# Packing gate columns and rank columns of an input projection into one weight tile

## The reference, cut to what matters

```
p_ctx = h_ctx @ w_in          # 256 x 1024 by 1024 x 3936
p_lat = h_lat @ w_in          # the same for the 256 tokens
u = concatenate([p_ctx, p_lat])
mq, mk, rr, rk, rv, mv, mo, gates, lw_f, lw_b, la, lg = split(u)
# widths: 7 x 512, gates 32, lw_f 64, lw_b 64, la 64, lg 128
li_f = gates[0] + b_i[0];   lf_f = log_sigmoid(gates[1] + b_f[0])   # 8 heads each
li_b = gates[2] + b_i[1];   lf_b = log_sigmoid(gates[3] + b_f[1])
a = sigmoid(a0 + la @ a_b_mat)       # la is the rank-64 input of this product
g = sigmoid(lg) @ g_b_mat            # lg is used for the 256 tokens alone
```

## Time and profile before

| | us |
|---|---|
| median of three runs | 2305.46 |
| lowest and highest run | 2303.93, 2309.15 |
| span of the profiled execution, first to last instruction | 2302.1 |
| TensorE busy in it | 2104.5 (91%) |
| VectorE, ScalarE, GpSimd busy | 793.3, 427.9, 38.1 |
| mean granted TensorE clock | 0.942 |

### The profile page before, as it was taken

The page is one execution under the profiler, slowest core; times in us unless marked ns, Lnnn a source line. Parts: engine busy times, 40 slices in busy tenths (PEclk is TensorE's granted clock), DMA queues, the critical chain, the costliest instruction groups (busy, mean ns, idle before and its releaser), DMA issues.

```text
span 2302.1 us, 31821 instructions
## 1 busy us (share of the span) xinstructions
PE 2104.5 (91%) x13702; PEld 1457.2 (63%) x13702; DVE 793.3 (34%) x1639; ACT 427.9 (19%) x892; POOL 38.1 (2%) x34
## 2 busy tenths in 40 slices
PE   6999886887899999999899899999898889999998
PEld 4554664677744444444575678887777778648844
DVE  3494488555411111111234345424674320001001
ACT  2200243221311111111233310003322110000001
POOL 1000200000000000000000000000000000000000
PEclk9999896688999999999998999999998889999999
DMA  9610004204579999999744278753300077899696
GB/s 311 244 37 1 1 1 148 74 2 161 198 323 426 427 422 428 427 428 425 271 153 175 73 274 324 275 214 110 111 1 2 1 276 273 312 394 345 247 345 239
DMA packets 161862, 511.95 MB, mean 222 GB/s; under 512 B 9022, under 2 KB 32269, under 8 KB 149069
## 3 DMA queue, kind: packets, MB, share of 16 engines
q1 hardware_dynamic: 146352, 480.51, 54.2%
q10 hardware_dynamic: 15389, 29.67, 3.5%
HBM read 509.11 MB, written 1.05 MB: 222 GB/s over the span
## 4 chain that ended last, share of the span: by engine, by line
PE 83%; DVE 7%; ACT 4%; DMA 3%; issue 2%; SPq 0%; POOL 0%; ACTq 0%; DVEq 0%; POOLq 0%
PE PS L388 35%; PE PS L2406 10%; PE PS L2427 5%; PE PS L2560 4%; PE PS L2321 4%; PE PS L2332 4%; PE PS L2245 3%; DMA work<-in_moe_w_gate_up_dram 2%; PE PS L2511 2%; PE PS L857 1%; PE PS L629 1%; PE PS L849 1%; PE PS L637 1%; PE PS L1668 1%; DMA work<-in_w_ada_dram 1%
## 5 line engine op out<-in xcount | busy, mean ns | idle before, releaser
L388 PE MATMUL PS<-hT,work 128*128 128x256 f32 x1456 | 329.0, 386 | 4.5 <-ACT hT L919 4.0
L388 PEld LDWEIGHTS PS<-hT,work 128*128 128x128 f32 x1456 | 278.4, 193 | 50.7 <-issue 10.1
L388 PE MATMUL PS<-work 128*128 128x256 f32 (+4 forms) x960 | 284.0, 457 | 2.4 <-DVE work L1976 1.5
L388 PEld LDWEIGHTS PS<-work 128*128 128x128 f32 (+2 forms) x960 | 178.6, 187 | 105.8 <-issue 78.3
L2406 PE MATMUL PS<-work,sq 128*64 128x512 f32 x1024 | 222.6, 592 | 1.3 <-ACT sq L2350 1.3
L388 PE MATMUL PS<-sq,work 128*128 128x128 f32 x1408 | 162.9, 280 | 11.7 <-DMA work<-in_moe_w_gate_up_dram 11.7
L388 PEld LDWEIGHTS PS<-sq,work 128*128 128x128 f32 x1408 | 162.5, 197 | 13.7 <-DMA work<-in_moe_w_gate_up_dram 12.7
L2406 PEld LDWEIGHTS PS<-work,sq 128*64 128x64 f32 x1024 | 76.0, 137 | 144.5 <-issue 144.5
L2427 PE MATMUL PS<-work 128*64 128x512 f32 x512 | 113.4, 595 | 12.0 <-ACT work L2444 12.0
L2560 PE MATMUL PS<-work 128*64 128x512 f32 (+1 forms) x352 | 114.4, 593 | 2.0 <-ACT work L2590 2.0
L2388 DVE COPY work<-PS 128x1024 f32<-128x1024 f32 x22 | 26.9, 1225 | 232.4 <-PE PS L2427 119.1
(11 more groups left out here) (584 smaller groups left out, 2304.9 us busy)
## 6 DMA issues: line engine op xcount, KB each, us to landing
work<-in_ex_gate_dram SPq DMA_DIRECT2D x32, 2048.0 KB, 12.3
work<-in_ex_up_dram SPq DMA_DIRECT2D x32, 2048.0 KB, 15.4
work<-in_ex_down_dram SPq DMA_DIRECT2D x32, 2048.0 KB, 11.0
work<-in_moe_w_gate_up_dram SPq DMA_DIRECT2D x32, 2048.0 KB, 10.6
work<-in_moe_w_down_dram SPq DMA_DIRECT2D x16, 2048.0 KB, 14.5
work<-in_ada_w_dram ACTq DMA_DIRECT2D x14, 2048.0 KB, 11.4
work<-in_moe_w_gate_up_dram SPq DMA_DIRECT2D x16, 1536.0 KB, 13.4
work<-in_ada_w_dram SPq DMA_DIRECT2D x10, 2048.0 KB, 11.6
```

The source lines that it names most:

```text
L388: ins = pe.matmul(outp, lhs, rhs, start=n == 0, stop=n == len(pairs) - 1, **kw)
```

## The change

The two gate copies and la's 64 weight columns are laid into one weight tile of 128 columns. It has four groups of 32 columns: input gates forward, input gates backward, forget gates forward, forget gates backward. The first 8 columns of a group are gate heads, the next 16 are a quarter of la's columns, the last 8 zeros. One product makes one output tile of 128 rows, and ScalarE reads it three times: rows 0 to 39 to li, rows 64 to 103 to lf, all 128 rows to la. A scale per row (1 on gate rows, 0 elsewhere) keeps the rank rows out of li and lf. `w_a` gets 128 rows, laid out like the tile with zeros on the gate rows and the padding, so that `la` in the new layout multiplies it directly; it is loaded by four DMAs of 16 rows, after a fill with zeros. The other two tiles stay as they are; `N_GATE` becomes 3, and counts that depend on it are renumbered.

```diff
-    w_a = sb("w_a", [C, H * C])
+    w_a = sb("w_a", [P, H * C])
-    w_gate = sb("w_gate", [P, KT, 2, 40])
+    w_gate = sb("w_gate", [P, KT, P])
-    gate_bias = sb("gate_bias", [40, 2])
+    gate_bias = sb("gate_bias", [P, 2])
-    for name, spec in (("w_in", ["act"] * 5 + ["dve"] * 20 + ["act"] * 8), ...
+    for name, spec in (("w_in", ["act"] * 3 + ["dve"] * 20 + ["act"] * 8), ...
-    N_GATE = 5
+    N_GATE = 3
-                act.dma_start(gate_bias[32 * d:32 * d + 8, j:j + 1], A[name]...)
+                act.dma_start(gate_bias[64 * j + 32 * d:64 * j + 32 * d + 8, 0:1], A[name]...)
-        ld(w_a[:, :], A["r_aB"][0])
+        sp.wait_ge(S["zeroed"], 4)
+        for g in range(4):
+            ld(w_a[32 * g + 8:32 * g + 24, :], A["r_aB"][0][16 * g:16 * g + 16, :])
-        eng.wait_ge(S["later"], 16 * 11)
+        eng.wait_ge(S["later"], 16 * 14)
     def stage0_pool():
-        pool.memset(w_gate[:, :, :, :], 0.0).then_inc(S["zeroed"], 1)
-        pool.memset(gate_bias[:, :], 0.0).then_inc(S["zeroed"], 1)
+        pool.memset(w_gate[:, :, :], 0.0).then_inc(S["zeroed"], 1)
+        po.link(pool.memset(gate_bias[:, :], 0.0))
+        for g in range(4):
+            po.link(pool.memset(gate_bias[32 * g:32 * g + 8, 1:2], 1.0))
+        pool.memset(w_a[:, :], 0.0).then_inc(S["zeroed"], 1)
     def gate_weights_pool():
-                ins = pool.tensor_copy(w_gate[:, :, j, 32 * d:32 * d + 8], w[:, :, 16 * d + 8 * j:16 * d + 8 * j + 8])
+                g = 2 * j + d
+                pool.tensor_copy(w_gate[:, :, 32 * g:32 * g + 8], w[:, :, 16 * d + 8 * j:16 * d + 8 * j + 8])
+                ins = pool.tensor_copy(w_gate[:, :, 32 * g + 8:32 * g + 24], w[:, :, 160 + 16 * g:160 + 16 * g + 16])
     def w_in_pe():
-        for j in range(2):
-            o = tile_begin("w_in", j)
-            product(o[0:40, :], [(w_gate[:, k, j, :], hall[:, k, :]) for k in range(KT)]).then_inc(S["tile_full"], 1)
+        product(tile_begin("w_in", 0), [(w_gate[:, k, :], hall[:, k, :]) for k in range(KT)]).then_inc(S["tile_full"], 1)
-        for j, (c0, m, t0, n) in enumerate(((32, P, 0, 2 * N), (160, C, 0, 2 * N), (224, P, N, N))):
+        for j, (c0, t0, n) in enumerate(((32, 0, 2 * N), (224, N, N))):
     def w_in_act():
-            evac(j, dst[0:40, :], tile_full(act, "w_in", j)[0:40, :], ACT.Identity, bias=gate_bias[:, j:j + 1])
-        evac(2, lw, tile_full(act, "w_in", 2), ACT.Tanh)
-        evac(3, la[0:C, :], tile_full(act, "w_in", 3)[0:C, :], ACT.Copy)
-        evac(4, lg, tile_full(act, "w_in", 4)[:, 0:N], ACT.Sigmoid)
+            rows_ = slice(C * j, C * j + R40)
+            act.activation(dst[0:R40, :], o[rows_, :], ACT.Identity, bias=gate_bias[rows_, 0:1], scale=gate_bias[rows_, 1:2])
+        evac(0, la, o, ACT.Copy)
+        evac(1, lw, tile_full(act, "w_in", 1), ACT.Tanh)
+        evac(2, lg, tile_full(act, "w_in", 2)[:, 0:N], ACT.Sigmoid)
     # two waits for tile 33 dropped beside a wait for the same count; emptied counts 2 -> 1, 13 -> by the list
-                product(o, [(w_a[:, p * P:(p + 1) * P], la[0:C, :])]).then_inc(S["tile_full"], 1)
+                product(o, [(w_a[:, p * P:(p + 1) * P], la)]).then_inc(S["tile_full"], 1)
```

More of the change, by code:

```diff
@@ L337, in build @@
     first_tile = {}
-    for name, spec in (("w_in", ["act"] * 5 + ["dve"] * 20 + ["act"] * 8), ("kap", ["act"] * 4), ("lora", ["act"] * 16),
+    for name, spec in (("w_in", ["act"] * 3 + ["dve"] * 20 + ["act"] * 8), ("kap", ["act"] * 4), ("lora", ["act"] * 16),
                        ("bonus", ["dve"] * 4), ("w_out", ["dve"] * 8), ("mla", ["act"] * 7 + ["dve"]),
@@ L420, in param_rows_act @@
                 row_loads[0] += 1
-                act.dma_start(gate_bias[32 * d:32 * d + 8, j:j + 1], A[name][0, d:d + 1, :].rearrange("a h -> h a"))\
+                act.dma_start(gate_bias[64 * j + 32 * d:64 * j + 32 * d + 8, 0:1], A[name][0, d:d + 1, :].rearrange("a h -> h a"))\
                    .then_inc(S["rows"], 16)
@@ L964, in w_in_pe @@
         pe.wait_ge(S["zeroed"], 5)
-        for j in range(2):
-            o = tile_begin("w_in", j)
-            product(o[0:40, :], [(w_gate[:, k, j, :], hall[:, k, :]) for k in range(KT)]).then_inc(S["tile_full"], 1)
+        product(tile_begin("w_in", 0), [(w_gate[:, k, :], hall[:, k, :]) for k in range(KT)]).then_inc(S["tile_full"], 1)
         w = unit(place["w_in", 7], KT, 352)
-        for j, (c0, m, t0, n) in enumerate(((32, P, 0, 2 * N), (160, C, 0, 2 * N), (224, P, N, N))):
-            o = tile_begin("w_in", 2 + j)
-            product(o[0:m, 0:n], [(w[:, k, c0:c0 + m], hall[:, k, t0:t0 + n]) for k in range(KT)])\
+        for j, (c0, t0, n) in enumerate(((32, 0, 2 * N), (224, N, N))):
+            o = tile_begin("w_in", 1 + j)
+            product(o[:, 0:n], [(w[:, k, c0:c0 + P], hall[:, k, t0:t0 + n]) for k in range(KT)])\
                 .then_inc(S["tile_full"], 1)
@@ L1032, in w_in_act @@
         act.wait_ge(S["rows"], 16 * row_loads[0])
+        o = tile_full(act, "w_in", 0)
         for j, dst in enumerate((li, lf)):
-            evac(j, dst[0:40, :], tile_full(act, "w_in", j)[0:40, :], ACT.Identity, bias=gate_bias[:, j:j + 1])
-        evac(2, lw, tile_full(act, "w_in", 2), ACT.Tanh)
-        evac(3, la[0:C, :], tile_full(act, "w_in", 3)[0:C, :], ACT.Copy)
-        evac(4, lg, tile_full(act, "w_in", 4)[:, 0:N], ACT.Sigmoid)
+            rows_ = slice(C * j, C * j + R40)
[3 more added lines that the diff above has]
+        evac(2, lg, tile_full(act, "w_in", 2)[:, 0:N], ACT.Sigmoid)
         ada_act(N_FIRST)
@@ L1088, in ml_pool @@
     def ml_pool():
-        pool.wait_ge(S["tile_full"], first_tile["w_in"] + 33)
         pool.wait_ge(S["tile_full"], first_tile["w_in"] + N_GATE + 28)
@@ L1095, in ml_gate_log_dve @@
     def ml_gate_log_dve():
-        dve.wait_ge(S["emptied_act"], 2)
+        dve.wait_ge(S["emptied_act"], 1)
         dve.scalar_tensor_tensor(out=g40(z_), in0=g40(lf), scalar=-1.0, in1=g40(lf), op0=ALU.mult, op1=ALU.max).then_inc(S["ml_args"], 1)
@@ L1188, in ml_tokens_dve @@
         dve.wait_ge(S["tile_full"], first_tile["w_in"] + N_GATE + 28)
-        dve.wait_ge(S["tile_full"], first_tile["w_in"] + 33)
         dve.tensor_tensor(diag[0:R40], over(ident[0:R40, 0:R40], 4), along(g40(decay), R40), ALU.mult)\
@@ L1469, in ml_out_dve @@
         dve.wait_ge(S["hn_std"], 3)
-        dve.wait_ge(S["emptied_act"], 13)
+        dve.wait_ge(S["emptied_act"], tile_owner[first_tile["w_in"] + N_GATE + 27][1])
         dv.link(dve.tensor_tensor(hm, hm, hv, ALU.mult))
```

## The result

| | before | changed |
|---|---|---|
| median of 20 executions each | 2308.21 us | 2300.73 us |
| lowest and highest | 2303.34, 2319.19 | 2292.46, 2308.84 |
| ratio of the changed to before | | 0.9959, 95% interval 0.9948 to 0.9970 |
| span of the profiled execution | 2302.1 us | 2299.1 us |
| mean granted clock in it | 0.942 | 0.938 |

The change makes the kernel 0.41% faster, 9.5 us by the ratio; 13.7 was forecast. The median of 2300.73 lies above the range of 2287.0 to 2297.0. With all executions of the study taken together (39 of the changed kernel, 117 of before) the means are 2299.8 and 2309.5 us, a difference of 9.7 with a standard error of 0.9.

A forecast was written before the change was run, and what follows sets the result against it. TensorE was taken to bound the input projection without a break. Span 2302.1 less 13.7 us of removed passes gives 2288.4; with 3.4 carried over to the median, 2291.7 us, range 2287.0 to 2297.0.

The forecast's parts named there:

- The work removed: Input projection on TensorE: two of four full-width passes, 32 load/matmul pairs, go; 13.7 us saved, bounds 13.5 and 13.8.
- What hides the added steps: Before and around the projection: added DMAs, fills, copies and readings stay under slack, 7.3 us for mq weights; nothing lost.
- the sign that copies or fills were not covered: TensorE's first projection matmul later than 49.6 us would mean the added GpSimd copies or fills delayed it.
- The scaled reading: ScalarE's li and lf readings with a per-row scale: between 0.68 us and twice that each, no change to the total.
- D: VectorE's convolution does not start earlier and holds TensorE; only the 2.2 us of slack is kept: 2303.3 us, chance 0.05.
- E: Four short w_a DMAs stall SP's queue, so mq weights come late and TensorE waits 19.9 us: 2311.6 us, chance 0.04.
- C: Wider weight loads are exposed in tile 0, costing 1.1 us, or 1.5 at low clock: 2293.2 us, chance 0.04.
- Later: After the projection: wider w_a products cost nothing, and events of the chain release the rest, so the gain stays whole.
- Rival B: Downstream of the projection, low-clock stretches fall differently, one costing 3.1 us: 2294.8 or 2288.6 us, chance 0.15.
- B's own sign: A gain of 13.7 us at 226 us that has become another number by 560 us.
- The sum's base: Whole kernel: the span of 2302.1 us, 3.4 below the runs' median of 2305.46, a difference carried over to the forecast.
- the rule on row groups: A weight load overlaps matmuls in flight only on different row groups, so the projection's wider load would add time.

The follow-up runs named there:

- e1: The changed kernel run again, unedited, against the kernel before: mean 2298.9 us, ratio 0.9964.
- e2: The changed kernel with the packed tile's product made three times, putting the 32 removed pairs back: mean 2307.2 us, ratio 0.9992 to before.
- e6: The kernel before plus 48 tiny products (96 pairs) ahead of the projection: mean 2315.2 us, ratio 1.0029 to before.
- e9: The changed kernel plus 16 tiny products placed behind the run of 256 tiny matmuls: mean 2300.7 us, ratio 0.9966 to before.
- e8: The kernel before plus 16 tiny products (32 pairs) ahead of the projection: mean 2321.8 us, ratio 1.0059 to before.
- e7: Only the gates packed, la kept as its own tile, plus 8 tiny products ahead of the projection: mean 2302.3 us, ratio 0.9966 to before.

## Why the prediction was wrong, point by point

**The work removed: right.** 15.25 us left the gate part, of which 1.0 is the first tile (50.22 to 59.15 is 8.93 us, against 9.92), where the clock rose earlier in this execution; the 14.2 that remain stand against the 13.7 taken. The rest is in what did not go: the lw tile took 7.07 us before and 6.81 after (59.15 to 65.96), the lg tile 3.61 and 3.42. Before, both followed a tile of another width; that this is the reason is a guess from these rows.

**What hides the added steps: right.** TensorE's first projection matmul came at 50.22 in place of 49.60, which the prediction names as the sign that copies or fills were not covered. But the delay is already there where the chain of the first norm begins, at 18.91 against 18.29 us, 20 us ahead of the copies, and in e1, the same program, the matmul came at 49.67. Loads, copies, fills and the queue stayed under their covers, and e2 shows them at no cost. The scaled reading was between its bounds, near the lower. VectorE never held TensorE. D and E did not happen; C neither: at the low clock the loads took 0.33 us with the pairs 0.85 apart, the same 0.85 as with the loads of 40 columns before.

**The step that failed** is the one under "Later": "The rest is released by events of the chain", with nothing found "that would swallow the gain". One thing is not released by an event: the next block of TensorE's own program, which comes by the count of its instructions. Removing 32 pairs moved every block end behind it. Of a gain of 14.0 us at 1564 us, 8.0 were left at the end in the mean of four traces; with the count put back, 13.5 of 14.3. Over all executions the gain is 9.7 us in place of 13.7, and 12.6 with the count put back. A row for it was there: the chain of the kernel before has a piece "issue" of 2.00 us at 369.96, in the middle of a plain run of matmuls with no wait in it. I read such pieces as nobody's, and asked only what waits for whom.

**Rival B** had the right region of causes and the wrong size. It priced a stretch at the lower clock at 3.1 us, by the first tile, where TensorE runs dense matmuls. In the delta-rule stage TensorE is on the chain with short bursts between waits, and one bad draw cost 11 us; the stop of 2 us ahead of it may make such a draw likelier. Over the fourteen traces the delta-rule stage up to the end of that stretch took 206 to 210 us in the six without a stop over 0.6 us in or just behind the run of tiny matmuls, mean 209.1, and 209.5 to 219.6 in the eight with one over 1.8, mean 214.7; three of the six had the stop at 1656 us. That the clock's fall is caused by the stop is argued from this, not shown; two of the eight (e6 and e9) had no slow stretch. B's own sign, another gain by 560 us, did show in the traces of the result: 14.6 us at 226, 17.9 at 560, and 13.3 at 700. In the mean of the four traces it is 13.7 at 558, so these were draws that cancel, and not the loss.

**The sum's base.** The median of three executions, 2305.46, was 4 us below the mean of all 117, 2309.5, and their spread of 5.2 us was taken for the kernel's; it is 4.3 as a standard deviation and 20 from end to end. By its own terms (2294.8 and 3.7 above) the range should have gone up to 2298.5, which 2300.73 misses too. Of the 9.0 us by which the median missed the forecast, 2.8 is the base (2308.21 against 2305.46 in the result) and 6.2 the gain that was missing between the medians; between the means 4.0 are missing.

**What adds up:** 13.7 us forecast; 9.7 (standard error 0.9) measured; 12.6 (1.1) with the block ends put back, and 7.2 of 6.9 for the half. What remains between 12.6 and 13.7 or 14.2 is within the error. How e8's 12.4 divides stays open, and so does whether a still better place for the ends exists.

## What to carry to other kernels

In a long unrolled program, an edit of instructions has a second effect besides its work: it moves the ends of the program's fetched blocks; in the kernels here whose ends idle products moved, that came with -4 (e7) to +12 us (e8) of 2300. Look in the chain for pieces marked "issue" within or just behind runs of very short instructions before the edit, and after it compare them. First rule out a DMA: a piece that ends just after the landing of a DMA that the code waits for there is a wait for data, whatever its mark says. A few idle tiny instructions in a wait can put the ends back. And take the base and the spread from many executions before forecasting a change of half a per cent.

## What the runs showed of the hardware

- TensorE stopped without a semaphore at fixed counts of its program, whole multiples of 256 loads and matmuls apart (128 float32 pairs) wherever the program runs straight; with a 16 KB packet on the instruction queue each time, it went on 2.2 to 3.0 us after the packet's start (57 stops in fourteen traces). The stop was what matmuls left uncovered of that, from nothing seen to 2.6 us (4.07 in e8).
- Behind the loop of the first expert stage it stopped for 1.5 to 2.5 us at the same place of the code in all fourteen traces, with such a packet 2.5 us ahead of the end (1123.8 to 1126.35 in before).
- The output width of a product of 512 columns didn't matter between 40 and 128 rows at either level of the clock: with a granted clock of 0.50 the loads of 40 columns took 0.19 us and those of 128 took 0.33, and the pairs stood 0.85 apart with both; with 1.00 the loads took 0.12 and 0.19, and the pairs stood 0.43 apart. This speaks against the rule on row groups weighed in the prediction (the Trainium skill, "TensorE: Matmul & The Clock Gate", "The mechanism"). The same section names a second case in which a load is pulled ahead, that it goes to a background weight buffer; no run here tells the two apart.
- ScalarE's reading of 40 x 512 from PSUM with bias and scale per row took 0.78 us, with the bias alone 0.68.
- The time of an execution goes with its mean granted clock: 15 us for 0.01 over 20 executions of the changed kernel (0.933 to 0.943, correlation -0.91).
